# Layer 1's first eight modulation chunks on VectorE in the dense blocks of a two-layer hybrid attention and expert encoder

## The reference, cut to what matters

```python
c_act = jax.nn.silu(c)                                  # c: (1, 1024)
for layer in range(2):
    mod = c_act @ ada_w[layer] + ada_b[layer]           # ada_w[layer]: 1024 x 6144
    sh_m, sc_m, g_m, sh_f, sc_f, g_f = split(mod, 6)
    h = rms_norm(x, norm_mix_g[layer]) * (1 + sc_m) + sh_m
    x = x + g_m * token_mixer(h, ...)                   # h @ w_in, attention, @ w_out
    h = rms_norm(x, norm_ffn_g[layer]) * (1 + sc_f) + sh_f
    y = swiglu(h, w_gate, w_up, w_down) if layer == 0 else moe_swiglu(h, ...)   # 8 experts, top 2
    x = x + g_f * y
return rms_norm(x, final_g)
```

## Time and profile before

| | |
|---|---|
| median of three runs | 1387.6 us |
| the profiled execution's own time | 1385.97 us |
| its span, first to last instruction | 1384.2 us |
| TensorE busy | 1311.0 us (95%) |
| VectorE busy | 417.2 us (30%) |
| ScalarE busy | 291.5 us (21%) |
| moved from and to HBM | 482.07 MB, mean 348 GB/s |
| matmuls with the experts' gate and up weights (L2505) | x4864, 481.8 us |
| matmuls with `ada_w` chunks (L2119), each chunk | x16 instructions, 1.92 us |

### The profile page before, as it was taken

How to read it: one execution, slowest core, us unless ns; L and a number is a source line. 1 busy time by engine, 2 the same in 40 slices (tenths; PEclk the granted TensorE clock), 3 DMA queues, 4 the chain that set the end, 5 groups by cost and what they waited for, 6 DMA issues and landing times.

```text
span 1384.2 us, 25418 instructions
## 1 busy us (share of the span) xinstructions
PE 1311.0 (95%) x11106; PEld 710.1 (51%) x11107; DVE 417.2 (30%) x792; ACT 291.5 (21%) x520; POOL 32.5 (2%) x82
## 2 busy tenths in 40 slices
PE   5999999999999999998779999999999999998996
PEld 4766888888768667341323433443343333443321
DVE  4876854444449656310100110001100111001001
ACT  3446544444424462100100000010010000010000
POOL 1002000000000020000000000000000000000000
PEclk9999999999999999998989999999999999999999
DMA  9988655555565799999999999999999999999996
GB/s 339 327 339 325 227 187 191 192 188 191 199 250 190 310 383 371 365 411 420 417 420 419 421 418 418 414 413 420 417 419 419 365 362 420 418 417 417 418 418 276
DMA packets 101691, 482.07 MB, mean 348 GB/s; under 512 B 9768, under 2 KB 11888, under 8 KB 67792
## 3 DMA queue, kind: packets, MB, share of 16 engines
q1 hardware_dynamic: 97632, 475.06, 86.2%
q10 hardware_dynamic: 2720, 2.93, 0.7%
q0 software_dynamic: 1232, 2.50, 0.7%
HBM read 477.32 MB, written 1.05 MB: 346 GB/s over the span
## 4 chain that ended last, share of the span: by engine, by line
PE 80%; DMA 10%; DVE 5%; SPq 2%; ACT 2%; issue 1%; POOL 0%; DVEq 0%; ACTq 0%
PE ps L2505 31%; PE ps L2548 14%; PE ps L2197 8%; PE ps L2199 8%; PE ps L2198 8%; DMA raw<-in_moe_w_down_dram 5%; DMA raw<-in_moe_w_up_dram 3%; DMA weights<-in_ada_w_dram 2%; PE ps L2119 2%; PE ps L2564 1%; DVE weights_lo L1294 1%; SPq L817 1%; PE ps L2479 1%; PE ps L2522 1%; PE ps L2278 1%
## 5 line engine op out<-in xcount | busy, mean ns | idle before, releaser
L2505 PE MATMUL ps<-raw,hX 128*32 128x512 f32 (+1 forms) x4864 | 481.8, 549 | 20.8 <-DMA raw<-in_moe_w_up_dram 14.4
L2505 PEld LDWEIGHTS ps<-raw,hX 128*32 128x32 f32 x4864 | 159.7, 111 | 318.3 <-issue 273.9
L2548 PE MATMUL ps<-raw,m_actT 128*32 128x512 f32 x1568 | 178.6, 596 | 6.0 <-DMA raw<-in_moe_w_down_dram 6.0
L2197 PE MATMUL ps<-weights_hi,hT_hi 128*128 128x512 f32 (+1 forms) x416 | 162.1, 390 | 2.6 <-DVE hT_lo L1397 1.4
L2199 PE MATMUL ps<-weights_hi,hT_lo 128*128 128x512 f32 (+1 forms) x416 | 159.0, 382 | 0.0
L2198 PE MATMUL ps<-weights_lo,hT_hi 128*128 128x512 f32 (+1 forms) x416 | 158.7, 381 | 0.0
L1688 DVE TENSOR_TENSOR m_act<-m_act,ps 128x512 f32<-128x512 f32 (+1 forms) x28 | 17.4, 621 | 436.4 <-PE ps L2505 435.6
L1294 DVE TENSOR_TENSOR weights_lo<-weights,weights_hi 128x2048 fp32r<-128x2048 f32 (+1 forms) x52 | 113.1, 2203 | 2.3 <-ACT weights_hi L978 1.1
L2548 PEld LDWEIGHTS ps<-raw,m_actT 128*32 128x32 f32 x1568 | 50.1, 110 | 115.2 <-issue 96.0
L978 ACT ACTIVATE weights_hi<-weights 128x2048 fp32r<-128x2048 f32 (+1 forms) x48 | 87.3, 1840 | 55.5 <-PE ps L2199 51.5
L2197 PEld LDWEIGHTS ps<-weights_hi,hT_hi 128*128 128x128 f32 x416 | 78.2, 188 | 21.0 <-issue 4.8
(11 more groups left out here) (277 smaller groups left out, 1054.1 us busy)
## 6 DMA issues: line engine op xcount, KB each, us to landing
raw<-in_moe_w_down_dram SPq DMA_DIRECT2D x96, 1024.0 KB, 17.4
raw<-in_moe_w_gate_dram SPq DMA_DIRECT2D x64, 1024.0 KB, 17.8
raw<-in_moe_w_up_dram SPq DMA_DIRECT2D x64, 1024.0 KB, 23.2
raw<-in_moe_w_gate_dram SPq DMA_DIRECT2D x64, 768.0 KB, 16.1
raw<-in_moe_w_up_dram SPq DMA_DIRECT2D x64, 768.0 KB, 16.7
weights<-in_ada_w_dram SPq DMA_DIRECT2D x18, 2048.0 KB, 9.9
raw<-in_moe_w_down_dram SPq DMA_DIRECT2D x32, 512.0 KB, 18.5
weights<-in_ffn_w_gate_dram SPq DMA_DIRECT2D x14, 1024.0 KB, 5.6
```

The source lines that it names most:

```text
L2197: pe.matmul(dst, stat_hi, hi, start=start, stop=False, skip_group_check=True)
L2505: mm = pe.matmul(ps[32 * q:32 * q + 32, bank, 0:COL[n]], hX[:, i, at32:at32 + 32], raw[buffer][:, at:at + COL[n]], start=(i == 0), stop=(i ...
L2548: mm = pe.matmul(ps[32 * quarter:32 * quarter + 32, bank, col:col + w], stationary[:, 32 * half:32 * half + 32], raw[buffer][:, D * j + w ...
```

## The change

Layer 1's chunks 0 to 7 leave TensorE. Each of the dense blocks 1 to 4 takes two of them, one through slot 1 and one through slot 2: SP loads them when the block's own weights in that slot are split, and loads the next block's weights into the slot when the chunk has been summed (`ada_summed`). VectorE multiplies each half of a chunk, 128x2048, by the activated `c` of its partition and adds it to `ada_acc` (`products`): four pairs of operations to a round, each pair in a place of its own, one before `turned(b, 1)` and one before `turned(b, 2)`. At the end of blocks 2 and 4 TensorE adds over the partitions with a matrix of ones (`sum_rows`, four matmuls to bank 7), and `mod_round` follows in blocks 3 and 5. `ADA_LATER[1]` keeps the chunks 8 to 11, in steps 0 to 3 of attention 1. All blocks use the halves of bank 6 for the transposes, so bank 7 is free. The loops over blocks are written out on all four queues. The `raw` buffers are first used in the order 0, 1, 3, 5 of their regions instead of 5, 0, 1, 3.

```diff
-ADA_LATER = [[(layer, n) for n in range(ADA_FIRST, ADA_CHUNKS)] for layer in range(DEPTH)]
-ADA_STEP = [0, 1, 2, 3, 4, 5, 6, 7]
-ADA_DENSE = [(1, n) for n in range(ADA_FIRST)]
+ADA_LATER = [[(0, n) for n in range(ADA_FIRST, ADA_CHUNKS)], [(1, n) for n in range(8, ADA_CHUNKS)]]
+ADA_STEP = [[0, 1, 2, 3, 4, 5, 6, 7], [0, 1, 2, 3]]
+ADA_BLOCKS = (1, 2, 3, 4)
+ADA_SLOTS = (1, 2)
...
-                with sp.Fori(0, NB) as j:
+                for j in range(NB):
                     for c in range(2):
+                        if c == 1:
+                            for n, slot in ada_of_block(j - 1):
+                                slot_split(slot, j)
+                                sp.dma_start(W[:, slot, :].rearrange("p (k n) -> p k n", k=2),
+                                             ada_v[1, n // 4, n % 4]).then_inc(w_loaded[slot], 16)
+                        before = [n for n, slot in ada_of_block(j - 1) if slot == c]
+                        if before:
+                            sp.wait_ge(ada_summed, before[0] + 1)
+                        else:
+                            slot_split(c, j)
...
+                def products(b, at):
+                    for n, slot in ada_of_block(b)[at:at + 1]:
+                        dve.wait_ge(w_loaded[slot], plan[("ada", 1, n)][2])
+                        if n == 4:
+                            dve.wait_ge(ada_rows, 1)
+                        for kk in range(2):
+                            k = 2 * (n % 4) + kk
+                            w, c = W[:, slot, kk * 2048:kk * 2048 + 2048], vcols[:, k:k + 1]
+                            if k == 0:
+                                a = dve.tensor_scalar(ada_acc[:], w, c, None, ALU.mult)
+                            else:
+                                a = dve.scalar_tensor_tensor(out=ada_acc[:], in0=w, scalar=c, in1=ada_acc[:],
+                                                             op0=ALU.mult, op1=ALU.add)
+                            if kk == 0:
+                                then(a)
+                        a.then_inc(ada_summed, 1)
+                        dve.wait_ge(ada_summed, n + 1)
...
                 def after(b):
+                    products(b, 1)
-                    turned(b, nu - 2, False)
+                    turned(b, nu - 2)
...
+                def sum_rows(r):
+                    pe.wait_ge(ada_summed, 4 * r + 4)
+                    if r:
+                        pe.wait_ge(mod_ready, 3 + r)
+                    for g in range(4):
+                        mm = pe.matmul(ps[32 * g:32 * g + 32, 7, :], ones[:, 0:32], ada_acc[:, 512 * g:512 * g + 512],
+                                       start=True, stop=True)
+                    mm.then_inc(ada_rows, 1)
...
-                    ada_chunk(*ADA_DENSE[0], 7)
...
-                    ada_chunk(*ADA_DENSE[3], 7)
```

More of the change, by code:

```diff
@@ L107 @@
 EARLY = 4
-FIRST_USE = tuple(2 * r + h for r in (5, 0, 1, 3, 2, 4, 6, 7, 8) for h in range(2))
+FIRST_USE = tuple(2 * r + h for r in (0, 1, 3, 5, 2, 4, 6, 7, 8) for h in range(2))
 SLOT_RANK = (0, 5, 1, 6, 3, 2, 7, 4)
@@ L365, in plan_ring @@
     for c, dmas in enumerate((2, 2, 1)):
-        loads[c] += 16 * dmas * NB
+        for b in ADA_BLOCKS:
+            for n, slot in ada_of_block(b):
+                if slot == c:
+                    plan[("ada", 1, n)] = (c, None, loads[c] + 16 * dmas * (b + 1) + ada_loads_before(c, b + 1))
+        loads[c] += 16 * dmas * NB + ada_loads_before(c, NB)
         holder[c] = ("split", FF_BASE[0] + PARTS * (NB - 1) + 2 * c + 2)
-    for (of, n), slot in zip(ADA_DENSE, ADA_DENSE_SLOT):
-        put(("ada", of, n), slot, ("ada", ADA_CHUNKS * of + n + 1))
     mixer(1, 0)
@@ L436, in build @@
         arg = place("arg", [P, 2, NT, HALF], F32, at + 16896)
+        ada_acc = place("ada_acc", [P, 2048], F32, at + 9216)
         sg = place("sg", [P, 2, HB], F32, at)
@@ L1077, in high_part @@
                 high(None, i // 2, i // 2, (i % 2) * PART, PART,
-                     b * per + (loads[i // 2] + per), b * PARTS + (base + i - 5))
+                     (b + 1) * per + loads[i // 2] + ada_loads_before(i // 2, b), b * PARTS + (base + i - 5))
             def dense():
@@ L1139, in dense @@
                 first()
-                with act.Fori(0, NB - 2) as j:
-                    before_last_units(j + 1, False)
-                    after(j + 1)
+                for b in range(1, NB - 1):
+                    before_last_units(b)
+                    after(b)
                 last()
@@ L1632, in before_last_units @@
                     gated(b, 0)
-                    for i in range(1, nu - 1):
-                        turned(b, i - 1, one_bank)
-                        gated(b, i)
+                    turned(b, 0)
+                    for r in range(2):
+                        if b == ADA_BLOCKS[2 * r + 1] + 1:
+                            mod_round(1, r)
+                    gated(b, 1)
+                    products(b, 0)
+                    turned(b, 1)
+                    gated(b, 2)
                 def last():
                     b = NB - 1
-                    before_last_units(b, True)
+                    before_last_units(b)
                     dense_out(0)
-                    mod_round(1, 0)
                     mean_square(2, 0)
-                    turned(b, nu - 2, True)
+                    turned(b, nu - 2)
                     normal(2, 0)
@@ L1655, in dense @@
                 first()
-                with dve.Fori(0, NB - 2) as j:
-                    before_last_units(j + 1, False)
-                    after(j + 1)
+                for b in range(1, NB - 1):
+                    before_last_units(b)
+                    after(b)
                 last()
@@ L2382, in after @@
                     gate_up(3, low_k, b, is_first)
[L2383 removed]
+                    turn(2, b)
                     gate_up(3, high_k, b, is_first)
                     down(2, (0,), b, is_first)
[L2386 removed]
+                    turn(3, b)
                     down(2, (1,), b, is_first)
                     down(3, (0, 1), b, is_first)
+                    for r in range(2):
+                        if b == ADA_BLOCKS[2 * r + 1]:
+                            sum_rows(r)
                 def last():
@@ L2416, in dense @@
                 first()
-                with pe.Fori(0, NB - 2) as j:
-                    one(j + 1)
+                for b in range(1, NB - 1):
+                    one(b)
                 last()
```

112 lines of the change are left out of this document (58 added, 54 removed).

## The result

| | before | after |
|---|---|---|
| median of the runs, us | 1387.3 (1385.3 to 1388.07, 4 runs) | 1376.24 (1374.79 to 1377.16, 4 runs) |
| profiled execution: own time / span, us | 1385.97 / 1384.2 | 1374.79 / 1373.0 |
| start of attention 1, us | 469.85 | 461.67 |
| from there to the experts' first matmul, us | 81.80 | 79.00 |
| experts' first matmul, us | 551.65 | 540.67 |

The ratio is 0.9922 (0.9906 to 0.9938): faster, by 11.1 us of the medians and 11.2 us of the two profiled executions. The forecast was 1377.5 us. The last two lines of the table say where it is: 10.98 us of it lie ahead of the experts.

A forecast was written before the change was run, and what follows sets the result against it. DMA bounds the kernel from about 470 us, TensorE's work mostly before; the end follows TensorE's start on the experts. -9.5 + 2.0 - 2.65, about -10.1 us, gives 1375.9 us profiled, a median of 1377.5 us; range 1372.0 to 1384.0 us.

The forecast's parts named there:

- The last dense block, -9.5: TensorE, last dense block: removing four chunks gains 3.65 us for the first and 1.95 us for each other, 9.5 us.
- Two sums, +2.0: TensorE, ends of dense blocks 2 and 4: each added sum over partitions costs 1.0 us, 2.0 us lost.
- The products, nothing: VectorE, two idle times per dense block: pairs of 4.6 us end 0.7 and 0.9 us before the low parts, costing nothing.
- Rival B: VectorE, dense blocks: products take 3.5 us each; 6 us lost, or 13 us with the first pair's too; chance 0.12, two halves.
- reading of the loads: Dense blocks: slot 1's chunk lands just when the first pair wants it, delay up to 0.7 us covered; slot 2's lands earlier.
- low part behind each pair still waits for ScalarE: Sign in the changed profile, dense blocks: behind every pair of products VectorE's low part should still wait for ScalarE.
- The down weights, 2.4 us to spare: Dense blocks: the down load goes out at 288.6 us, lands 7.7 us later, 2.4 us before it is due; nothing lost.
- rival A: Dense blocks: down weights land 5.0 us late in four blocks, 20 us lost, 1397.5 us; chance 0.07.
- Attention 1, -2.65: Chunks out of steps 4 to 7: 0.8 us from step 4, 1.85 from step 5, nothing from 6 and 7; 2.65 us gained.
- The bytes, nothing: Crowded stretch before the experts: four chunks fewer, 8.4 MB or 20 us of DMA, give nothing.
- the tie: 550 to 570 us: expert weight loads wait for TensorE, so the end moves as much as TensorE's start on the experts.
- Loops, nothing: Writing out the loops over dense blocks, together with the transposes in one bank and the buffer order, costs or gains nothing.

The follow-up runs named there:

- dense_only: Changed kernel with only blocks 1 and 2 taking chunks (four); layer 1's other eight in attention 1, steps 0 to 7: 1378.43 us, ratio 0.9946.
- longer_first: Changed kernel with an added 2048-element maximum on VectorE behind the slot 1 products in dense blocks 1 to 4: 1378.28 us, one run.
- down_late: Changed kernel with the down weights' load of blocks 2 to 5 held until VectorE's low parts of the next block's first quarter: 1401.59 us, one run.
- bytes_back: Changed kernel with four unread 2 MB loads of ada_w put back ahead of the first expert chunks: 1376.53 us, ratio 0.9929.
- steps_0167_again: steps_0167 run again, in a later sitting beside the changed kernel: 1374.94 us, ratio 0.9915, five runs.
- filler_67: Changed kernel with 14 unread identity multiplications on TensorE behind each of steps 6 and 7 of attention 1: 1377.82 us, ratio 0.9939.
- written_out: Kernel before with only its loops over the dense blocks written out on four engines: 1386.53 us, ratio 0.9999.
- steps_0167: Changed kernel with its four attention 1 chunks in steps 0, 1, 6 and 7 instead of 0 to 3: 1374.41 us, ratio 0.9913.
- steps_4567: Changed kernel with its four attention 1 chunks in steps 4 to 7 instead of 0 to 3: 1378.15 us, one run.
- no_attn_chunks: Changed kernel with one short matmul left of each of chunks 8 to 11, loads kept: 79.02 us from attention's start to experts; 2095.92 us, routing changed.
- longer_second: Changed kernel with an added 2048-element maximum on VectorE behind the slot 2 products in dense blocks 1 to 4: 1380.78 us, one run.

## Why the prediction was right, point by point

- **The last dense block, -9.5.** From the first load behind its own weights (364.15 us before, 365.94 us after) to the in-projection's matmuls it takes 36.71 us where it took 46.62: -9.9 us. The 0.4 us more than predicted are the price of the later chunks: between neighbouring transposes the second had cost 2.06 us, the third and fourth 4.22 us together, where the starts next to them gave 1.95 us each. dense_only has the same gain by itself.
- **Two sums, +2.0.** 1.09 us each, so 2.2 us, near the lower bound. Blocks 2 and 4 take 35.0 and 34.9 us, blocks 1 and 3 the 33.9 us of before.
- **The products, nothing.** A pair is 4.73 us (4.6 predicted), 0.94 us of wait is left behind the second (0.9 predicted). The duration taken from the nearest in size, 2.28 us, was near the measured 2.35; the proportion of the earlier trace rows, 3.5 us, was wrong. The Trainium skill's formula ("VectorE: DVE Perf Modes", on the errata) gave 2.29 us for an operation on two tensors; longer_first's maximum of two tensors took 2.29 us, so it holds for its form, and a product and sum with a scalar was 0.06 us longer. Rival B was priced by the two longer kernels: 2.3 us more in each pair would have cost 5.3 us in the second places and 1.5 us in the first, 6.8 us if the two add up, beside the 6 us of its first half. The first place keeps 1.73 us in block 3, which begins a sum and where the first product is only 1.28 us long, 0.72 us in block 1, which begins one too but waits 0.92 us for its chunk, and 0.58 us (0.7 predicted) in block 2. In block 4 nothing is kept, since the chunk came 1.08 us late and the cover was 0.7 us. Here the prediction's reading of the loads was too good, and its sign that the low part behind each pair still waits for ScalarE failed once in eight. What saved the block is what the prediction named for this case, the half of `gate_up(2)` ahead of `down(1)`.
- **The down weights, 2.4 us to spare.** Landing 7.5 us (7.7 predicted), no wait, 2.5 us to spare by the changed kernel's own rows. down_late showed that rival A's wait is real: 25.7 us for a load some 7.5 us later in four blocks.
- **Attention 1, -2.65.** -2.80. Its two parts are right as well: ScalarE's copy 0.94 us earlier (0.8 predicted), the scores behind it 1.85 us more (1.85 predicted), and nothing from steps 6 and 7: VectorE's last maximum is 2.79 us earlier.
- **The bytes, nothing, and the tie.** bytes_back confirms the first. For the tie, the experts began between 540.4 and 567.3 us in the profiles of the changed kernel and its variants that route as it does, and in nine of the thirteen comparable profiles, both kernels' included, 831.9 to 832.7 us followed, whether the start came early or late. In four it was more: 833.05 us (steps_0167_again), 833.73 (filler_67), 835.26 (written_out) and 835.45 (steps_0167). What makes this stage longer in some executions is open; it isn't tied to the start, since written_out and steps_0167 start where their like do.
- **Loops, nothing.** written_out confirms it; the transposes' bank and the order of buffers were not tried alone.

The sum at the experts' start is -9.9 + 2.2 - 2.8 = -10.5 us, and 10.98 us were measured there. The median lies 1.45 us above the profiled execution (1.6 predicted). The 0.4 us left over at the experts' start stand ahead of block 1, whose first load is at 151.07 us instead of 151.52; in the profiles of all the kernels here it lies between 150.8 and 152.3 us, so it is most likely no effect of the change.

What the prediction left out was TensorE's clock. I took a chunk for mere work, to be gained or not. It is also what keeps TensorE busy: the chunks of steps 0 and 1 that the change leaves in place hold the clock in that stretch (steps_4567, no_attn_chunks), and where it empties steps 4 to 7 the clock held in four profiles of this very timeline (the changed kernel twice, longer_second, down_late) and fell in two (bytes_back, longer_first), for 2.6 and 1.4 us. So a forecast that took the clock for granted was also lucky: a fall would have taken back up to 2.6 of the 11 us in the profile. How often it falls in the changed kernel isn't known. Nor is it shown that such falls make up the spread of its single times. The kernel before spreads as much, with a clock of 1.00 in attention in both of its profiles, and the two slow executions that were profiled (1377.95 us of steps_0167, 1388.81 us of written_out) had lost their time behind the experts' start.

## What to carry to other kernels

When the end of a kernel is tied to when one engine reaches a stage, sum only what lies on that engine's path up to there, and look for the tie itself: free bandwidth ahead of it bought nothing here. Work moved into an idle time is free up to the idle time's end, which the row behind it names; ask of each place, and of each turn of a loop, what stands right behind it, since 2.3 us more cost nothing in one block and 1.0 us in another at the same place, and 1.3 us in the other place. A load that feeds such a place uses up the cover too when it is late. Before taking work away from TensorE in a stage where it already waits, ask whether that work holds its clock: in two kernels here the clock took back most of what the missing matmuls would have saved.

## What the runs showed of the hardware

- TensorE's granted clock fell to 0.50 for some 8 us (steps_4567) behind stretches in which it had been busy for 2.00 and 1.31 of 4 us, and not in the same stretches filled by two chunks of 1.92 us. Behind a stretch of 2.05 of 4 us it fell in some executions and not in others, though TensorE's timelines ahead were alike to 0.01 us: 1.4 us (longer_first), 2.6 us (bytes_back) or nothing (after). In steps_0167_again it fell in the second of two stretches of 3.03 and 3.09 of 4 us, and in steps_0167 it held through the same ones.
- A load of 2 MB landed 7.5 us after its issue when nothing else was under way, and 8.7 to 9.8 us after it when it followed another 2 MB about 4 us later (the changed kernel, blocks 1 to 4).
- A product and sum of 2048 float32 elements with a scalar of its own for each partition took 2.35 us, against 2.28 us for the difference of two tensors of that size, and 1.28 us for the product with a scalar alone.
- The sums over partitions, eight matmul instructions of 512 columns in four groups of 32, cost 1.09 us between the starts of their neighbours, 0.14 us each, where the dense matmuls of 512 columns start 0.23 us apart.
